# One projection ahead of the compressed keys and values: reordering a sparse attention's front end on one core

## The reference

```
z  = rms_norm(x, kv_norm) @ kv_w            # 256 x 768: raw k, raw v, selected k, v, window k, v
                                             # (2 groups of 64 in each)
ks, kw = rope(rms_norm(z_k, gain))           # selected and window keys, per group
for name in ("k", "v"):                      # compressed keys and values
    blocks = raw_name[16n : 16n + 32] + pe   # n = 0..14, each block 32 tokens x 64 numbers
    hidden = gelu(blocks @ w1)               # w1: 2048 x 256, both groups: 30 rows
    out    = hidden @ w2                     # w2: 256 x 64
kc = rope(rms_norm(out_k, kc_gain));  vc = out_v

y  = rms_norm(x, b_norm) @ b_w_in            # 256 x 1072: 16 heads of 64, and 48 gates
q  = rope(rms_norm(y[:, :1024], q_gain));  gates = sigmoid(y[:, 1024:] + b_gate)
out = sum over the three kinds (compressed, selected, window) of gate * attention(q, k, v)
x = x + out @ b_w_out
```

## Time and profile before

| | us |
|---|---|
| median of 3 runs | 2927.88 |
| lowest, highest | 2927.32, 2928.37 |
| profiled execution | 2929.42 |
| its span | 2927.6 |

### The profile page before, as it was taken

How to read it: one execution, slowest core, us unless ns; L and a number is a source line. 1 busy time by engine, 2 the same in 40 slices (tenths; PEclk the granted TensorE clock), 3 DMA queues, 4 the chain that set the end, 5 groups by cost and what they waited for, 6 DMA issues and landing times.

```text
span 2927.6 us, 31365 instructions
## 1 busy us (share of the span) xinstructions
PE 2418.8 (83%) x12811; PEld 2054.3 (70%) x12811; DVE 1984.4 (68%) x2430; ACT 1416.6 (48%) x1367; POOL 28.0 (1%) x52
## 2 busy tenths in 40 slices
PE   4837799883575999999999999968569985667898
PEld 3736699762554888888888888856459975544898
DVE  6555744656464888888888888865448865444787
ACT  5322443432332777777767777753344332244442
POOL 0000000000000000000000000000000000000000
PEclk9957899986677999999999999989689985666999
DMA  8400755741042999999999999983114541200453
GB/s 328 162 1 24 243 184 186 271 149 53 1 156 84 365 347 346 355 356 358 356 355 340 355 357 355 356 264 121 52 66 159 187 152 59 96 1 24 148 186 113
DMA packets 293719, 590.72 MB, mean 202 GB/s; under 512 B 11702, under 2 KB 86564, under 8 KB 292928
## 3 DMA queue, kind: packets, MB, share of 16 engines
q1 hardware_dynamic: 289872, 572.33, 55.0%
q0 software_dynamic: 3696, 16.32, 1.8%
HBM read 587.56 MB, written 1.05 MB: 201 GB/s over the span
## 4 chain that ended last, share of the span: by engine, by line
PE 59%; DVE 6%; ACT 1%; DMA 1%; issue 1%; POOL 0%; DVEq 0%; SPq 0%; ACTq 0%
PE ps L1108 17%; PE ps L1110 17%; PE ps L1109 17%; PE ps L1188 2%; PE ps L1173 1%; PE ps L1310 1%; DVE arena L1760 1%; DVE arena L1616 1%; PE ps L1293 1%; PE ps L1271 1%; DVE arena L1784 1%; PE ps L1145 1%; PE ps L1162 1%; PE ps L1211 1%; DVE Z L1625 0%
## 5 line engine op out<-in xcount | busy, mean ns | idle before, releaser
L778 ACT ACTIVATE w_hi<-raw 128x2048 fp32r<-128x2048 f32 x548 | 1041.9, 1907 | 621.5 <-PE ps L1110 507.3
L1601 DVE TENSOR_TENSOR w_lo<-raw,w_hi 128x2048 fp32r<-128x2048 f32 x548 | 1224.9, 2274 | 54.4 <-ACT w_hi L778 38.2
L1108 PE MATMUL ps<-w_hi,xT_hi 128*128 128x512 f32 (+3 forms) x1600 | 636.7, 398 | 43.2 <-DVE xT_lo L1706 24.8
L1110 PE MATMUL ps<-w_hi,xT_lo 128*128 128x512 f32 (+3 forms) x1600 | 623.0, 389 | 0.0
L1109 PE MATMUL ps<-w_lo,xT_hi 128*128 128x512 f32 (+3 forms) x1600 | 622.7, 389 | 0.0
L1108 PEld LDWEIGHTS ps<-w_hi,xT_hi 128*128 128x128 f32 x1600 | 306.2, 191 | 109.9 <-DVE xT_lo L1706 26.2
L1109 PEld LDWEIGHTS ps<-w_lo,xT_hi 128*128 128x128 f32 x1600 | 306.6, 192 | 62.1 <-issue 3.3
L1110 PEld LDWEIGHTS ps<-w_hi,xT_lo 128*128 128x128 f32 x1600 | 305.8, 191 | 62.3
L1108 PE MATMUL ps<-xT_hi,w_hi 128*128 128x256 f32 (+1 forms) x1120 | 323.6, 289 | 15.3 <-DVE xT_lo L2292 11.0
L1109 PE MATMUL ps<-xT_lo,w_hi 128*128 128x256 f32 (+1 forms) x1120 | 323.3, 289 | 0.0
L1110 PE MATMUL ps<-xT_hi,w_lo 128*128 128x256 f32 (+1 forms) x1120 | 323.2, 289 | 0.0
(11 more groups left out here) (314 smaller groups left out, 1970.6 us busy)
## 6 DMA issues: line engine op xcount, KB each, us to landing
raw<-in_moe_w_gate SPq DMA_DIRECT2D x112, 1024.0 KB, 5.3
raw<-in_moe_w_up SPq DMA_DIRECT2D x112, 1024.0 KB, 5.3
raw<-in_moe_w_down SPq DMA_DIRECT2D x112, 1024.0 KB, 5.3
raw<-in_w_ada SPq DMA_DIRECT2D x48, 1024.0 KB, 5.1
raw<-in_f_w_up SPq DMA_DIRECT2D x44, 1024.0 KB, 5.0
raw<-in_f_w_down SPq DMA_DIRECT2D x22, 1024.0 KB, 4.8
raw<-in_w_in SPq DMA_DIRECT2D x20, 1024.0 KB, 5.7
raw<-in_a_w_in SPq DMA_DIRECT2D x12, 1024.0 KB, 5.1
```

The lines of the kernel that those rows point to most:

```text
L778: act.activation(w_hi[:, k % HI, 0:LEN[k]], raw[:, r, 0:LEN[k]], ACT.Copy).then_inc(w_hi_ready, 1)
L1108: pe.matmul(out_, lh, rh, start=start, stop=False)
L1110: return pe.matmul(out_, ll, rh, start=False, stop=stop)
L1601: dve.tensor_tensor(w_lo[:, k % RAW, 0:LEN[k]], raw[:, k % RAW, 0:LEN[k]], w_hi[:, k % HI, 0:LEN[k]].bitcast(F32), ALU.subtract).then_inc( ...
```

## The change

The projection of the queries moves from behind the compressed keys and values to a place ahead of them, and their work is laid between its column groups. In detail:

- `ORDER` becomes "kv", "nsa_in", "kc", "vc", so the weight stream changes with it. Both gain vectors are loaded one behind the other (`gain_n`), and one root serves both norms. VectorE scales `X` a second time with `gain_n` right behind the first `to_columns`, and TensorE makes the second set of columns right behind `linear("kv")`, into PSUM banks 4 to 7.
- `linear` gets a `between`. TensorE: the raw transposes of k and v behind group 0 (`raw_columns`), the eight transposes of the selected and window keys behind group 1 (`key_columns`). VectorE: adding the position numbers and splitting the blocks of both behind the drain of group 0 (`blocks`).
- k and v have buffers of their own. The keys' norms and ropes take both token blocks in one instruction, and one root serves both kinds; the queries' squares, root and rope also take both token blocks at once. The work beside a root (`overlapped`) stands between sending and waiting.
- In the first layer the blocks (30 columns, split into `aT_hi` and `aT_lo`) are stationary and the weights move, 256 columns at a time: 2 x 8 x 3 = 48 matmuls for each of k and v. The hidden rows come out as 30x256, so gelu runs on them and four small transposes with two ScalarE copies are added (`hid`, `hid_tr`, `hid_cols`).

The weight stream and GpSimd's loads:

```
-                 "fa_in", "fa_out", "conv0", "kv", "kc", "vc", "nsa_in", "nsa_out", "conv1"]
+                 "fa_in", "fa_out", "conv0", "kv", "nsa_in", "kc", "vc", "nsa_out", "conv1"]
...
+            load(gain_n, a["b_norm_2"][0].partition_broadcast(P), ld_gain)
+            pool.wait_ge(cmp_free, got(cmp_free))
-            for n in "kv":
-                pool.wait_ge(cmp_free, got(cmp_free))
+            for i, n in enumerate("kv"):
...
-            gain_row(a["b_norm_2"][0])
```

On ScalarE:

```
             linear("kv")
+            to_columns(bank=4)
+            root(stat_a[:, 0:8])
+            upto(BASE["nsa_in"] + 3)
+            for i in range(2):
                 act.wait_ge(raw_tr, got(raw_tr))
+                act.activation(rawT[i], ps[:, 4 + i, :], ACT.Copy).then_inc(raw_sb, 1)
+                act.activation(peT[i], ps[:, 6 + i, 0:16], ACT.Copy).then_inc(raw_sb, 1)
+            upto(BASE["nsa_in"] + 4)
+            copy_heads(kvT.rearrange("p n t -> p (n t)"), [(4, 512), (5, 512)], P)
+            for i in range(2):
                 act.wait_ge(blk_ready, got(blk_ready))
+                act.activation(blk_hl[i][0], blk32[i].rearrange("p l n -> p (l n)"), ACT.Copy).then_inc(blk_hi, 1)
             linear("nsa_in")
```

On TensorE:

```
             linear("kv")
+            to_columns(H, bank=4)
...
+            linear("nsa_in", between={0: raw_columns, 1: key_columns})
...
                 for part in range(2):
                     hi, lo = slot(8)
-                    for c in range(2):
-                        for k in range(8):
-                            lpair = 8 * part + k
-                            last = three(ps[:, 4 + c, 0:2 * N_CMP], hi[:, k, c * P:(c + 1) * P],
-                                         lo[:, k, c * P:(c + 1) * P], bh[:, lpair, :], bl[:, lpair, :],
-                                         lpair == 0, lpair == 15)
+                    for k in range(8):
+                        lpair = 8 * part + k
+                        last = three(ps[0:2 * N_CMP, (6, 4)[i], 0:256], bh[:, lpair, :], bl[:, lpair, :],
+                                     hi[:, k, :], lo[:, k, :], lpair == 0, lpair == 15)
+                    last.then_inc(w_used, 1)
```

On VectorE:

```
+            linear("nsa_in", into_rows(zn), between={0: blocks})
+            tt(mix[:, :, :], z[:, :, 0:D], z[:, :, 0:D], ALU.mult)
+            step(dve.tensor_reduce(stat_a, mix[:, :, :].rearrange("p b (h d) -> p (b h) d", d=HD), AX.X, ALU.add))
+            upto(BASE["vc"] + 1)
+            inv_root(stat_a, stat_a, HD)
...
+            rope_of(q, cos2, sin2, nrope)
+            upto(BASE["vc"] + 1 + 2)
+            dve.wait_ge(cmp_out, got(cmp_out))
```

More of the change, by code:

```diff
@@ new lines, in raw_columns @@
+            def raw_columns():
+                pe.wait_ge(dup_ready, got(dup_ready))
+                pe.wait_ge(ld_cmp, 64)
+                for i in range(2):
+                    for g in range(2):
+                        for b in range(TB):
+                            pe.transpose(ps[:, 4 + i, g * T + b * P:g * T + (b + 1) * P],
+                                         rawdup[i][:, b, g * P:(g + 1) * P], ident)
+                    pe.transpose(ps[:, 6 + i, 0:16], pe_rows[i], ident[0:16, 0:16]).then_inc(raw_tr, 1)
@@ new lines, in key_columns @@
+            def key_columns():
+                pe.wait_ge(heads_ready, got(heads_ready))
+                pe.wait_ge(raw_sb, got(raw_sb, 4))
+                for i in range(4):
+                    for b in range(TB):
+                        last = pe.transpose(ps[:, 4 + i // 2, (i % 2) * T + b * P:(i % 2) * T + (b + 1) * P],
+                                            ks_twice[:, i // 2, b, i % 2].rearrange("p s d -> p (s d)"), ident)
+                last.then_inc(heads_tr, 1)
+            linear("nsa_in", between={0: raw_columns, 1: key_columns})
@@ L1564, in _ @@
-            z = zrows(NSA_DIM)
+            pe.wait_ge(kc_normed, got(kc_normed))
+            for g in range(2):
+                last = pe.transpose(ps[:, 1, g * 16:g * 16 + N_CMP],
+                                    kc_twice[:, g].rearrange("p s d -> p (s d)"), ident[0:N_CMP, 0:N_CMP])
+            last.then_inc(kc_tr, 1)
+            pe.wait_ge(kc_sb, got(kc_sb))
             pe.wait_ge(heads_ready, got(heads_ready))
@@ new lines, in _ @@
+            for i in range(2):
+                for side in range(2):
+                    step(dve.tensor_copy(
+                        rawdup[i].rearrange("p b (g s d) -> p b g s d", g=2, s=2)[:, :, :, side, :],
+                        blocked_rows(zk[:, :, i * P:(i + 1) * P], 2)))
+            beat().then_inc(dup_ready, 1)
+            dve.wait_ge(dup_ready, sent(dup_ready))
+            keys = [blocked_rows(zk[:, :, c0:c0 + P], 2) for c0 in (256, 512)]
+            for i, x in enumerate(keys):
+                tt(kv_sq[:, i], x, x, ALU.mult)
@@ L2323, in _ @@
+            rope(kc_n, 2, 8, cosc[0:N_CMP, :], sinc[0:N_CMP, :], crope, N_CMP)
+            step(dve.tensor_copy(kc_twice, twice(kc_n, [N_CMP, 2, 2, HD])))
+            beat().then_inc(kc_normed, 1)
+            dve.wait_ge(kc_normed, sent(kc_normed))
             beat().then_inc(heads_ready, 1)
```

272 lines of the change are left out of this document (131 added, 141 removed).

## The result

| | before | after |
|---|---|---|
| median, us | 2927.6 | 2854.03 |
| lowest, highest | 2923.31, 2928.37 | 2848.98, 2856.66 |
| profiled execution | 2929.42 | 2856.66 |
| its span | 2927.6 | 2854.8 |

The new kernel is faster: the ratio is 0.975, with a 95% interval of 0.9731 to 0.9768. Forecast were 2857.6 us and 2850 to 2868. The profiled executions differ by 72.8 us where 70.3 were forecast. Attention and last layers took 366.0 us behind the changed stretch, before 365.2.

The account below looks back on a forecast made before the run. The old stretch was taken as a chain with one engine working at a time. Steps summing to 68.5 us plus 1.0 for the gain replace 139.8, 70.3 less: 2859.1, less 1.5 to the median, 2857.6 us; range 2850 to 2868.

Parts of the forecast that it names:

- b, group 0: First column group of the queries' projection: 48 matmuls at 0.22 to 0.23 us, full clock, 10.95 us.
- e, hand-over: Wait added between group 1 and group 2 of the queries, for VectorE's split of the 384-column slot: 4.6 us.
- f, group 2: Last group of the queries' projection, 48 matmuls of 48 columns, all at the low clock: 10.25 us.
- g, to the root: VectorE from group 2 to the queries' root, becoming the bound with TensorE's first layers hidden under it: 11.0 us.
- i, two splits: Two more VectorE splits behind the queries' rope, before hidden beside the projection: 4.55 us.
- j, compressed keys: End of the stretch, from the compressed keys' copy through signals, two transposes and a copy: 4.5 us.
- k, gain: VectorE's first norm waits for both gain rows; the second was taken to cost 1.0 us.
- 1, TensorE bound and low: First layers' 96 matmuls stay at 0.42 us, 40 us in all: 20 us lost, 2878 us; chance 4%.
- 2, gains one behind the other: The two gain rows' loads follow each other at the first norm: +3.1 us, 2860.7; chance 15%.
- 3, low clock at group 0: Queries' first group starts with ten low-clock matmuls: +2.0 us, 2859.6; with late first layers +5.0, 2862.6; chance 25%.
- 4, full clock through group 2: The queries' last group keeps the full clock: up to 4.9 us less, 2852.7; chance 15%.
- 5, a low clock in the last dense layers: Clock does not rise in the last dense layers: up to 145 us more, 3003 us, slower than before; chance 1%.

Follow-up runs that it names:

- e_weights_stationary: The changed kernel, but in the first layers of k and v the weights are stationary again and 30 columns move; 2878.41 us, ratio 0.9829.
- e_blocks_before_keys: The changed kernel, but ScalarE makes the blocks' high parts before it copies the transposed key blocks; 2852.69 us, ratio 0.9744.
- e_k_layer_twice: The changed kernel with the first layer of k multiplied a second time into a bank that nothing reads; 2859.99 us, ratio 0.9751.
- e_out_splits_late: The changed kernel, but VectorE's two splits for the output projection stand behind the signal that starts the attention; 2850.24 us, ratio 0.9736.
- e_filled_gap: The changed kernel with 48 unread matmuls of 512 columns on TensorE while it waits for the norm ahead of kv; 2857.05 us, ratio 0.9752.
- e_all_five: The kernel of e_all_four with 42 unread matmuls on TensorE in the wait ahead of kv; 2846.23 us, ratio 0.9716.
- e_all_four: The changed kernel with high parts before key copies, one more slot split ahead of them, separate gain waits and late output splits; 2844.87 us, run again 2839.16.

## Why the prediction was right, point by point

**Total.** 3.6 us too high. The stretch was forecast at 68.5 us without the gain and measured at 66.9. Of the 2.5 us between the forecast gain and that of the profiled executions, the stretch is 1.6 and the gain's term 1.2; 0.5 lies ahead of the X addition, and 0.8 behind the attention's start goes the other way. Each step, from the rows above (a to j run from 2421.86 to 2488.79):

| step | forecast | measured | |
|---|---|---|---|
| a, second columns | 3.1 | 2.8 | four subtractions in 2.48 |
| b, group 0 | 10.95 | 11.0 | full clock |
| c, ten transposes | 1.2 | 1.4 | full clock |
| d, group 1 | 10.95 | 11.0 | no wait |
| e, hand-over | 4.6 | 4.6 | 2448.11 to 2452.70 |
| f, group 2 | 10.25 | 9.1 | until 2461.82 |
| g, to the root | 11.0 | 10.85 | VectorE bound |
| h, queries | 7.4 | 7.4 | until 2480.09 |
| i, two splits | 4.55 | 4.4 | |
| j, compressed keys | 4.5 | 4.3 | |
| k, gain | +1.0 | +1.7, and -1.9 | see below |

**What bounds it.** Right: before, the stretch was a chain, and the new order with its batched norms and ropes is worth 49.9 us by e_weights_stationary. The hand-over e was named as the new wait, with its length and its releaser (`w_lo`), and e_blocks_before_keys shows the cause by removing it. VectorE as the bound from g on is shown by e_k_layer_twice, where the doubled layer, 5.6 us more of TensorE, cost 1.8, and by e_out_splits_late, where 4.4 us less of VectorE gave 4.2.

**f, mis-sized.** I took all 48 matmuls at the low clock. The first 11 ran 0.11 us apart, then the clock fell at 2453.9 and the rest took 0.21: 9.1 us. Ten or eleven full matmuls stand in five other executions with this wait; in e_filled_gap and e_k_layer_twice the group was low from its first matmul and took 10.2 us, the forecast's value. With no such wait ahead the group kept 2.4 GHz to its end in e_blocks_before_keys and e_all_five, and to its last four or five matmuls in e_all_four and e_all_four_2.

**g, right in size.** The 96 matmuls of the first layers took 13.8 us: until 2467.5 at the low clock 0.21 us each, then 0.115. They end well before VectorE needs them, as forecast. The position numbers' additions (four of 64x240, 2.4 us, for k and again for v) were within the bounds of 3.0 and 6.1 and hidden: VectorE waits 5.79 us behind them.

**k, the step that failed.** The second gain cost 1.7 us, not 1.0: the wait is 5.85 us, over the 5.2 that the text named as wrong. Still nothing of it reached kv's drain, since kv, started later, found the full clock and its first group took 11.05 us for 13.0 before. So the sum had an error of 0.7 in one term and missed another of -1.9 altogether; that the two leave -0.2 is luck, and nothing in the prediction foresaw it. The prediction priced the clock ahead of group 0 and of group 2, but took kv's own start as the same in both programs.

**Rivals.** 1, TensorE bound and low: did not happen, yet e_weights_stationary shows that its mechanism was real for the old form, 22.9 us. 2, gains one behind the other: 1.7 us lies between sharing nothing (0.5) and full sequence (4.1). 3, low clock at group 0: did not happen; ahead of group 0 stood sixteen transposes and 2 us of rest, and group 0 began at full clock. 4, full clock through group 2: a fifth of it (11 of 48 matmuls); whole only in e_blocks_before_keys and e_all_five, where the wait ahead was gone. 5, a low clock in the last dense layers: no; the same 1287 matmuls ran from 2662 to 2843:

```profile
2662.00:2843.00 181.00, 181.00 (x1287) 170.81 (x1287) 147.40 (x184) 68.55 (x52) 0.00 (x0) 1.00 0.47 157
```

**The transposes and the clock.** The rows of 2402 to 2406 above show the clock rising to 1.00 while TensorE had run nothing but sixteen transposes since the convolution: a mean of 0.82 over 2402 to 2404 puts the rise ahead of 2403, and kv starts at 2403.94. It did so in six of the twelve executions with an unfilled gap, and in the other six it rose only inside kv. The Trainium skill, page "TensorE: Matmul & The Clock Gate", Part 4 on transposes, says that transposes do not count as busy and do not engage the full clock. These rows disagree with it in half of the cases; why only in half is open. The trace lists these transposes as MATMUL and does not show whether the mode that the page speaks of is on.

## What to carry to other kernels

Look for stretches in which one engine works at a time, and put the independent product between the steps of the chain; here that, with the batching that came with it, was worth 50 us, over twice what the cheaper operation gave. When a matmul moves few columns, count weight loads instead of columns and make the narrow operand the stationary one. After a reordering, read what stands behind each waiting instruction: two instructions in the wrong order on ScalarE and two early splits on VectorE were worth another 8 us in the stretch.
